# Half of the first norm's shift as a bias of the input products: a hybrid attention and convolution block on one core

## The reference, cut to what matters

```python
mods_x = split(silu(c) @ w_mod + b_mod, 6)          # shift, scale, gate, twice; (2048 x 12288)
nx = rmsnorm(x, g) * (1 + scale_x) + shift_x        # latent tokens
nc = rmsnorm(ctx, g) * (1 + scale_c) + shift_c      # context tokens
q_a, kv_a, k_rope, g_b, g_c, hh = split(nx @ w_in)  # 512, 256, 64, and 3 x 1024 columns
pc = nc @ w_in[:, 512:832]                          # kv_a and k_rope of the context
q = rmsnorm(q_a, g_q) @ w_q_b ; kv = rmsnorm(kv_a, g_kv) @ w_kv_b
o_conv = g_b * conv3(g_c * hh)                      # short convolution, width 3
```

## Time and profile before

| | |
|---|---|
| time, median of 3 runs | 1109.44 us (1107.96 to 1110.99) |
| span of the profiled execution | 1107.5 us; the page has no time of its own for it beside the span |
| busy: PE, DVE, ACT, POOL | 1011.4, 549.5, 221.2, 20.3 us |
| granted TensorE clock | full nearly throughout |
| loads | 380.30 MB, mean 343 GB/s |
| stages | to 121 us: loads run at 388 GB/s, modulation and input products; to 146 us: last set and sums of squares; to 319 us: convolution loop; then attention and output; from about 572 us the experts |

### The profile page before, as it was taken

How to read it: one execution, slowest core, us unless ns; L and a number is a source line. 1 busy time by engine, 2 the same in 40 slices (tenths; PEclk the granted TensorE clock), 3 DMA queues, 4 the chain that set the end, 5 groups by cost and what they waited for, 6 DMA issues and landing times.

```text
span 1107.5 us, 15664 instructions
## 1 busy us (share of the span) xinstructions
PE 1011.4 (91%) x6004; PEld 566.6 (51%) x6005; DVE 549.5 (50%) x1082; ACT 221.2 (20%) x442; POOL 20.3 (2%) x28
## 2 busy tenths in 40 slices
PE   3889999999999889999998999998899898998985
PEld 2534578888885345444485645433334333344421
DVE  3000186854824694985582234545246344545524
ACT  5211110000002363010341213222113112213212
POOL 0000000000002001000000000000000000000002
PEclk9899999999999999999999999999999998999998
DMA  9999979999854747999739999999999999999994
GB/s 358 389 389 389 377 232 359 372 345 328 284 181 169 256 144 262 387 387 335 230 130 367 371 405 403 406 408 407 409 409 406 408 407 408 409 407 408 409 406 180
DMA packets 158359, 380.30 MB, mean 343 GB/s; under 512 B 10498, under 2 KB 44112, under 8 KB 157136
## 3 DMA queue, kind: packets, MB, share of 16 engines
q1 hardware_dynamic: 158288, 379.35, 91.3%
HBM read 377.22 MB, written 2.10 MB: 342 GB/s over the span
## 4 chain that ended last, share of the span: by engine, by line
PE 64%; DMA 13%; SPq 12%; DVE 6%; issue 2%; ACT 2%; POOL 0%; ACTq 0%; DVEq 0%; POOLq 0%
PE ps L654 64%; DMA ring<-in_w_exp_down 7%; SPq L537 4%; SPq L532 4%; DVE part L1590 3%; DMA ring<-in_w_exp_up 2%; DMA ring<-in_w_in 1%; DMA ring<-in_w_mod 1%; DMA qnT<-in_w_mod 1%; SPq L397 1%; DVE tiny L1736 1%; SPq L417 1%; DVE xres L2021 1%; SPq L394 1%; SPq L395 0%
## 5 line engine op out<-in xcount | busy, mean ns | idle before, releaser
L654 PE MATMUL ps<-nreg,ring 128*128 128x256 f32 (+2 forms) x1312 | 306.9, 398 | 6.7 <-DVE ring L1741 4.1
L654 PEld LDWEIGHTS ps<-nreg,ring 128*128 128x128 f32 (+1 forms) x1312 | 243.8, 190 | 63.1 <-issue 30.8
L1590 DVE SCALAR_TENSOR_TENSOR part<-ring,csT,part 128x512 f32<-128x512 f32 x232 | 174.7, 753 | 8.6
L654 PE MATMUL ps<-ring,nreg 128*32 128x512 f32 (+1 forms) x1344 | 174.2, 602 | 3.6 <-DMA ring<-in_w_exp_up 3.2
L654 PE MATMUL ps<-ring,conv 128*32 128x512 f32 (+2 forms) x688 | 104.5, 663 | 23.0 <-DMA ring<-in_w_exp_down 22.1
L654 PE MATMUL ps<-ring 128*128 128x512 f32 x256 | 110.7, 592 | 0.0
L654 PEld LDWEIGHTS ps<-ring,nreg 128*32 128x32 f32 (+1 forms) x1344 | 49.1, 115 | 111.7 <-issue 111.6
L2021 DVE TENSOR_TENSOR xres<-xres,ps 128x512 f32<-128x512 f32 x96 | 61.6, 683 | 48.9 <-PE ps L654 48.9
L654 PEld LDWEIGHTS ps<-ring 128*128 128x128 f32 x256 | 48.6, 190 | 60.4 <-issue 60.0
L654 PEld LDWEIGHTS ps<-ring,conv 128*32 128x32 f32 (+2 forms) x688 | 30.2, 125 | 88.4 <-issue 83.9
L654 PE MATMUL ps<-pick,qnT 128*128 128x128 bf16 x384 | 67.8, 221 | 2.8 <-DMA ring<-in_w_exp_up 2.8
(11 more groups left out here) (265 smaller groups left out, 883.9 us busy)
## 6 DMA issues: line engine op xcount, KB each, us to landing
ring<-in_w_mod SPq DMA_DIRECT2D x78, 1024.0 KB, 10.9
ring<-in_w_exp_gate SPq DMA_DIRECT2D x128, 512.0 KB, 13.6
ring<-in_w_exp_up SPq DMA_DIRECT2D x128, 512.0 KB, 15.1
ring<-in_w_exp_down SPq DMA_DIRECT2D x128, 512.0 KB, 14.4
ring<-in_w_in SPq DMA_DIRECT2D x12, 2048.0 KB, 13.4
ring<-in_w_out SPq DMA_DIRECT2D x8, 2048.0 KB, 11.6
ring<-in_w_mod SPq DMA_DIRECT2D x3, 2048.0 KB, 19.7
ring<-in_w_in SPq DMA_DIRECT2D x3, 1664.0 KB, 15.7
```

The lines of the kernel that those rows point to most:

```text
L654: return nc.tensor.matmul(o, l, r, start=start, stop=stop)
L1590: ins = V.scalar_tensor_tensor(out=out_, in0=w_, scalar=scale, in1=acc_, op0=ALU.mult, op1=ALU.add)
```

## The change

Groups are loaded and taken in another order: `MOD_ORDER` was 0, 4, 1, 5, 2, 6, 3, 7 and becomes 4, 5, 6, 2, 7, 3, 0, 1. The scale of chunks 0 to 7 is there early, their shift (groups 0 and 1) last. For these chunks `nT` is only scaled before the input products; the missing shift is multiplied with the same 832 columns (`shift_products`, 16 matmuls; `bias_columns`, 7), and the result is added as a per-partition bias where the products are read from PSUM: raw `q_a` is copied to `q_raw`, its squares and gains take the bias, and so do those of `kv_a` and `k_rope`, which are handled in two halves since latent and context tokens have different biases. VectorE then adds the shift to `nT[:, 0:8, 0:T]` for the convolution. Sets s = 2 and 3 keep scale and shift in one step. `load_conv(0, 0)` is issued in front of the last group, after `q_full` (the first query block of the last set). The first pass of the convolution loop is written out: block (0, 0, m=0) is begun with chunks 8 to 15 and ended with 0 to 7 around the shift products, and the sums of squares (`in_squares`) stand behind block (0, 0, m=1).

```diff
-        MOD_ORDER = [g for s in range(4) for g in (s, s + 4)]
+        MOD_ORDER = [4, 5, 6, 2, 7, 3, 0, 1]
+        LATE = 2
...
-            for s in range(1, 4):
-                for n in (2 * s, 2 * s + 1):
-                    load_early(n)
-                if s == 1:
-                    sp.wait_ge(mod_rows, 1)
-                load_in(s)
...
+            sp.wait_ge(mod_rows, 1)
+            load_in(1)
+            load_early(2)
+            load_in(2)
+            load_early(3)
+            load_early(4)
+            load_in(3)
...
-            sp.wait_ge(mod_rows, 7)
+            load_early(5)
+            load_early(6)
+            sp.wait_ge(q_full, 1)
             load_conv(0, 0, CONV0 + CW)
+            load_early(7)
             load_group(8, 12, mslot, freed_by_pe)
-            sp.wait_ge(q_full, 1)
+            sp.wait_ge(shift_full, 2)
             load_conv(0, 1, CONV0 + 2 * CW)
             load_conv(0, 2, CONV0)
...
+            for s in range(1, SETS):
+                query_set(s, range(4))
+                step_group(2 * s)
+                kv_set(s, 0)
+                mod_cols_of(2 * s, 0, 7)
+                step_group(2 * s + 1)
                 rotary_set(s)
...
+                mod_cols_of(2 * s + 1, 1, 7)
                 kv_set(s, 1)
...
+            def shift_products():
+
+                pe.wait_ge(shift_ready, LATE)
+                pe.wait_ge(q_sq, 4)
+                for bank, at, end in ((2, 0, QL), (3, QL, WI)):
+                    for k in range(4 * LATE):
+                        ins = mm(ps[32 * (k % 4):32 * (k % 4) + 32, bank, 0:end - at], shift_cols[:, k, :],
+                                 wiq[k // 4][:, k % 4, at:end], k < 4, k >= 4 * LATE - 4)
+                    ins.then_inc(shift_full, 1)
...
+            def in_squares():
+
+                pe.wait_ge(q_sq, 8)
+                for m in range(4):
+                    ins = mm(ps[:, 7, 0:T], ones, q_squ[:, T * m:T * m + T], m == 0, m == 3)
+                ins.then_inc(stat_full, 1)
+                pe.wait_ge(kr_sum, 1)
+                mm(ps[:, 6, :], cst[:, C_DUP:C_DUP + P], krs[:, :], True, True)
+                mm(ps[:, 7, T:2 * T], cst[:, C_ROTK:C_ROTK + P], krs[:, 0:T], True, True).then_inc(kr_mm, 1)
+                pe.wait_ge(kv_out, 1)
+                pe.wait_ge(kv_sq, 2)
+                for m in range(2):
+                    ins = mm(ps[:, 4, :], ones, squ[:, 1024 + 512 * m:1536 + 512 * m], m == 0, m == 1)
+                ins.then_inc(stat_full, 1)
...
+            pe.wait_ge(w_full[0], 16 * 3)
+            pe.wait_ge(q_sq, 2)
+            first_conv(range(4 * LATE, KC))
+            shift_products()
+            first_conv(range(4 * LATE))
+            bias_columns()
+            conv_blocks(0, 0, BANKS_C, (1,))
+            in_squares()
+            conv_blocks(0, 1, BANKS_H)
+            pe.wait_ge(kv_out, 2)
+            mod_sum_cols(8, 0)
+            pe.wait_ge(gc_out, 2)
+            pe.wait_ge(mean_wide, 2)
+            conv_blocks(0, 2, BANKS_B)
+            mod_sum_cols(9, 1)
+            with pe.Fori(1, 4) as i:
...
             kv_gain(0)
-            ve.wait_ge(stat_q, 1)
+            ve.wait_ge(stat_full, 1)
+            ve.wait_ge(kr_mm, 1)
+            ve.wait_ge(q_out, 4)
             mean_square_wide(rowq, ps[:, 7, 0:T], QL)
```

More of the change, by code:

```diff
@@ L718, in first_rows, with rows_T @@
                     ins.then_inc(mod_rows, 1)
-            def rows_T(rows, done, side):
-                for j in range(KC // 2):
+            def rows_T(rows, done, banks, js):
+                for j in js:
                     if j >= 3:
@@ L732, in _ @@
             pe.wait_ge(xs_ready, 2)
[L733 removed]
+            rows_T(xs, xT_lat, LAT_BANKS, range(KC // 2))
             pe.wait_ge(small_done, 1)
[L735 removed]
+            for k in range(KC):
                 first_rows(0, k)
             pe.wait_ge(ctxs_ready, 2)
[L738 to L740 removed]
+            pe.wait_ge(xT_lat, KC // 2)
+            rows_T(ctxs, xT_ctx, CTX_BANKS, range(3))
             mod_cols_of(FIRST, 0, 7)
[L742 to L747, removed]
+            rows_T(ctxs, xT_ctx, CTX_BANKS, range(3, KC // 2))
             def query_set(s, ms):
@@ L778, in step_group @@
                 group_rows(n, 7)
[L780 to L787, removed]
+            query_set(0, (0, 2))
+            pe.wait_ge(xT_ctx, KC // 2)
+            query_set(0, (1, 3))
+            pe.wait_ge(modT_done, 1)
+            for k in range(KC):
+                first_rows(1, k)
@@ L793, in _ @@
                 kv_set(s, 1)
[L794 to L804, removed]
@@ new lines, in bias_columns @@
+            def bias_columns():
+                pe.wait_ge(shift_out, 2)
+                for m in range(6):
+                    mm(ps[:, 7, 384 + 2 * m:386 + 2 * m], shift_rows[:, 128 * m:128 * m + 128], sum4[:, 0:2], True, True)
+                mm(ps[0:64, 7, 396:398], shift_rows[:, KR0:WI], sum4[:, 0:2], True, True).then_inc(shift_full, 1)
+            def in_squares():
[11 more added lines that the diff above has]
+                ins.then_inc(stat_full, 1)
@@ L1281, in _ @@
             for m in range(4):
                 sc.wait_ge(q_full, m + 1)
-                nc.scalar.activation(squ[:, T * m:T * m + T], ps[:, m, 0:T], ACT.Square).then_inc(q_sq, 1)
+                copy(q_raw[:, m, :], ps[:, m, 0:T]).then_inc(q_sq, 1)
+            for n in (6, 7):
+                rows_out(n, 7, n % 2, False)
+            for n in range(2):
+                sc.wait_ge(shift_full, n + 1)
+                at, end, bank = ((0, QL, 2), (QL, WI, 3))[n]
+                copy(shift_rows[:, at:end], ps[:, bank, 0:end - at]).then_inc(shift_out, 1)
@@ L1284, in _ @@
+            sc.wait_ge(shift_ready, LATE + 1)
+            for m in range(4):
+                sc.wait_ge(q_sq, m + 1)
+                nc.scalar.activation(q_squ[:, T * m:T * m + T], q_raw[:, m, :], ACT.Square, bias=in_bias[:, m, 0:1])\
+                    .then_inc(q_sq, 1)
             sc.wait_ge(kr_full, 1)
-            copy(krs[:, :], ps[:, 6, :]).then_inc(kr_sum, 1)
+            for v in range(2):
+                ins = nc.scalar.activation(krs[:, T * v:T * v + T], ps[:, 6, T * v:T * v + T], ACT.Identity,
+                                           bias=in_bias[:, 6, v:v + 1])
@@ L1287, in kv_square @@
+            ins.then_inc(kr_sum, 1)
             def kv_square(m):
                 sc.wait_ge(kv_full, m + 1)
-                nc.scalar.activation(squ[:, 1024 + 512 * m:1536 + 512 * m], ps[:, 4 + m, :], ACT.Square).then_inc(kv_sq, 1)
+                for v in range(2):
+                    ins = nc.scalar.activation(squ[:, 1024 + 512 * m + T * v:1280 + 512 * m + T * v],
+                                               ps[:, 4 + m, T * v:T * v + T], ACT.Square, bias=in_bias[:, 4 + m, v:v + 1])
+                ins.then_inc(kv_sq, 1)
@@ new lines, in _ @@
+                    ins.then_inc(nT_lat, 1)
+            for s in range(LATE):
+                shift_of(6 + s, shift_cols[:, 4 * s:4 * s + 4, 0:2]).then_inc(shift_ready, 1)
+                ve.wait_ge(shift_ready, s + 1)
+                ve.wait_ge(mod_rows, 2 * s + 3)
+                for k in range(4 * s, 4 * s + 4):
+                    V.tensor_scalar(nT[:, k, 0:T], nT[:, k, 0:T], shift_cols[:, k, 0:1], None, ALU.add).then_inc(nT_shift, 1)
+            ve.wait_ge(shift_full, 3)
+            V.tensor_copy(tiny[:, 16:28], ps[:, 7, 384:396])
```

147 lines of the change are left out of this document (84 added, 63 removed).

## The result

| | before | after |
|---|---|---|
| time, median | 1109.5 us (1107.96 to 1110.99, 4 runs) | 1122.0 us (1120.48 to 1123.26, 4 runs) |
| span of the profiled execution | 1107.5 us | 1120.3 us |
| second pass of the convolution loop begins on TensorE | 189.53 | 199.83 |

The account below looks back on a forecast made before the run. Loads bound the kernel to 105.9 us, then TensorE to 371. VectorE's late group 8 and TensorE's two waits put the second pass at 196.5, 7.0 us later: 1109.4 + 7.0 = 1116.4 us, range 1110 to 1122.

Parts of the forecast that it names:

- its two places: TensorE's waits for VectorE at the first and second `mod_sum_cols` of the first convolution pass: 7.2 and 1.9 us.
- The last quarter lands at 126.5: Front loads: 7808 KB behind the quarter landed at 105.9 take 20.6 us at 388 GB/s.
- margin of 2.3 us: Load queue: `load_conv(0, 0)` is issued at 108.0, before the bytes ahead of it have landed at 110.3.
- Worse: Rival, chance 0.16: the load queue runs dry before `load_conv(0, 0)`, costing 3 to 6 us: 1119 to 1122.
- The load decides: At the last quarter TensorE is ready at 122.7, nearly 4 us early, so its landing sets the time.
- 25.0 from quarter to `in_squares`: TensorE's work from the last quarter, shift products and bias columns included, sums to 25.0 us; `in_squares` begins at 151.5.
- Group 8 at 166.6: VectorE starts group 8 of the first pass at 166.6, 14.0 us later than before.
- 7.2 us of wait at the first closing: TensorE reaches the first `mod_sum_cols` at 171.9 and waits until VectorE finishes group 8 at 179.1.
- 1.9 at the second: TensorE reaches the second `mod_sum_cols` at 193.7 and waits 1.9 us for `sum_out(8)`, which ends at 195.6.
- hidden to within 0.1: Slow clock behind the first wait costs TensorE 1.9 us, which the wait at the second closing covers.
- the 196 to 199 that were to show it: Sign in the changed profile: the second pass of the convolution loop starts at 196 to 199.
- Carried to the end one to one: What is lost before the convolution loop's second pass, 7.0 us, reaches the end unless something behind gives way.

Follow-up runs that it names:

- e4: Kernel before the change plus eight unused reciprocals on VectorE ahead of its loop, delaying group 8: ratio 1.0084 to the kernel before.
- e2: Changed kernel with the first closing (group 8) moved behind the last two convolution blocks of the first pass: ratio 1.0112 to the kernel before.
- e3: Changed kernel with the first convolution weights issued behind the last group instead of in front of it: ratio 1.0057 to the kernel before.
- e7: Changed kernel with 16 more matmuls, result unread, in place of the long wait at the first closing: 1121.8 us.
- e5: Changed kernel with the edits of e1 and e3 together: ratio 1.0007 to the kernel before, over 12 runs.
- e1: Changed kernel with the sums of squares ahead of block (0, 0, m=1) instead of behind it: ratio 1.0077 to the kernel before.
- e6: e5 with the first pass's second closing moved behind the first block of the second pass: ratio 1.0012 to the kernel before, over 12 runs.
- e8: e6 with convolution block (0, 0, m=1) cut in three to fill the waits in the sums of squares: ratio 1.004 to the kernel before.

## Why the prediction was right, and where it was too small

The direction, the mechanism and its two places were right; e4, e2 and e3 show them one by one. The size was 12.5 instead of 7.0. That puts 1122.0 outside the forecast's own 1114 to 1119 and on the upper edge of the range of 1110 to 1122; that it is not beyond the edge is luck. By the steps:

- **The last quarter lands at 126.5**: 127.9. The step that failed is the margin of 2.3 us in the rival "Worse". The issue time was right: `load_conv(0, 0)` went out at 107.61 (108.0 predicted). But 110.3, where the bytes in front of it were to end, was counted back from a landing, and a landing comes later than its bytes: from 127.25 on next to nothing moves (8 GB/s and less) and from 126 to 127 only 111 GB/s, while the last quarter lands at 127.9. The margin was 0.5 us of queued bytes, and from the issue it took over 2 us until the rate was back (354 GB/s from 110 on). The 1.45 us lost there are all of the 1.4. Around it the 388 GB/s held. That rival came true in part, with a smaller price than its 3 to 6 us. "The load decides" was right; e3, without load and gap in front, prices both at 4.9 us.
- **25.0 from quarter to `in_squares`**: 153.73 - 127.89 = 25.8. Shift products 2.9 (predicted 2.8), bias columns 1.5 (1.4), the rotary set and kv block as taken. The first matmuls of the quarter took 1.46 instead of 0.9, at a granted clock of 0.50 (126 to 127.9), a price that the prediction didn't have; the rest is handovers.
- **Group 8 at 166.6**: 168.94. The 2.3 are 1.4 of landing, 0.8 of that sum and 0.1 behind. From `in_squares` on it was 15.1 predicted and 15.2 measured.
- **7.2 us of wait at the first closing**: 7.16. **1.9 at the second**: none; TensorE reaches it at 199.02, 1.1 us after `sum_out(8)`.
- **The clock "hidden to within 0.1"**: this step failed. The price was 2.6 instead of 1.9, since the closing itself, four tiny matmuls (recorded twice), runs at the low clock too (1.70 for 0.81). So TensorE comes to the second closing behind VectorE and not ahead of it, and some 1.0 of the 2.6 is not hidden; e7 takes the low clock away and gives back 0.86. With the 2.3 of the late start this makes 10.3 instead of 7.0 at the second pass, which at 199.83 lies outside the 196 to 199 that were to show it.
- **Carried to the end one to one**: the 10.3 was still 10.3 at 404.90, and 12.8 at the end. Of the 2.5 us in between, 1.75 came in attention, behind a wait after which the clock fell, and 0.75 in the experts' stage, where TensorE waited 1.1 us longer for its loads (`exp_up`, 7.2 against 6.1). The last section says why I do not give them to the change.

Nor did the change win anything on TensorE: it reaches the first closing at 174.52, before at 174.01, and 171.9 was predicted; 2.3 of the difference are the late start again. e5 shows what is left without the two mistakes of order: VectorE still starts 8.1 us later, which uses up the slack, and the kernel takes the time of before. None of the versions tried was faster than before.

## What to carry to other kernels

A step that leaves the path in front can lengthen the one behind it: before work is taken off a load-bound front, write down how much slack each wait of the next stage has (here 8.9 and 7.0 us), and see how late the other engine begins. When the last piece of a stage decides, nothing that is not needed by it may stand in the queue in front of it, which was 4.9 of the 10.3 us here, and the lead of a load that waits for a computation is counted in bytes still to move, not from a landing: here 2.3 us by the count were 0.5 in the trace, and 1.45 us of loading were lost. And filling a wait helps only if it is the wait of the engine that is late; else it comes back further on, with the clock's price on top.

## What the runs showed of the hardware

- **The granted clock at a wait of about 2 us is not fixed.** In attention TensorE waits 2.17 or 2.18 us for VectorE in every kernel. In before, e1, e2, e4, e5 and e7 the clock stayed up and the four matmuls (x8) took 1.96 to 1.97; in after, e3, e6 and e8 it fell and they took 3.1 to 3.6. The kernel before, and after:

```profile
394.60 1.96 PE L654 MATMUL ps<-nreg,ring 128*128 128x256 f32 x8 [2.17 <-DVE ring L1741]
```

```profile
404.90 3.30 PE L665 MATMUL ps<-nreg,ring 128*128 128x256 f32 x8 [2.18 <-DVE ring L1837]
...
406.30:408.30 2.00, 2.00 (x6) 1.64 (x5) 1.96 (x4) 0.01 (x1) 0.00 (x0) 0.50 0.45 78
```

  The program is the same there, and e3, with the low clock, is faster than e1, without it. The Trainium skill (TensorE: Matmul & The Clock Gate, Part 1: The HAM clock gate) says that the window over which the hardware watches TensorE's activity is free-running and does not restart with the kernel. That the same wait has both outcomes fits this; no run here shows that it is the reason. By the end of attention the fall had cost 1.4 to 1.8 us. Even 1.45 us can be enough: behind that wait at the second closing the clock fell in e1, at a cost of 1.7 us, and stayed up in e5. Each kernel has one profiled execution, so how often it falls in each stays open.
- **The price of a long wait is paid by the small instructions too.** Behind 7.16 us of idle the clock was 0.50 for some 5 us, which cost 2.6 us, against 1.9 behind the 2.46 us of the earlier trace rows; the closing's share is 0.9. The price does not follow the length of the wait: behind the 5.81 us of e4 the clock was low for 8 us, which cost 4.0.
- **Four strips of 32 weight columns gave nearly the whole factor of four in the shift products too.** The 16 matmuls of 512 and 320 columns took 2.93 us from start to start, near the 2.8 that came from the earlier trace rows. At full width they would take 11.2 (an estimate from the 0.86 of the prediction), so the factor is 3.8. The Trainium skill (TensorE: Matmul & The Clock Gate, Measured speedup vs the span model) gives 2.38, for three strips; that factor would have made 4.7 (an estimate), which the trace does not bear out for four.
- **The experts' first stage differs between kernels that have the same code there.** From the attention wait named above to the first `nreg,ring` row of x32 in the experts' loop (607.38 in before) it took 212.8 us in before, 215.6 in after (1.75 of it the clock), 210.3 in e5 and 216.1 in e7; TensorE's waits for `exp_up` were 6.1, 7.2, 4.5 and 8.0. Whether the loads' lead at the end of the convolution decides that was not tried.
